# Pages ahead of the other loads in SyncE's queue, page products in halves around a step's clip, prepares at steps 14 and 18

## What is computed

```python
def stick_breaking_block(q, k, v, bias, q_pos, k_pos):
    z = (jnp.einsum('bqhd,bkhd->bhqk', q, k).astype(jnp.float32) * (SB_HEAD_DIM ** -0.5)
         + bias.astype(jnp.float32)[None, :, None, None])
    mask = k_pos[None, :] < q_pos[:, None]
    log_keep = jnp.where(mask, jax.nn.log_sigmoid(-z), 0.0)
    between = lax.cumsum(log_keep, axis=3, reverse=True) - log_keep
    a = jnp.where(mask, jnp.exp(jax.nn.log_sigmoid(z) + between), 0.0)
    return jnp.einsum('bhqk,bkhd->bqhd', a.astype(v.dtype), v)
...
    past_k = cache_sb_k[:, page_table].reshape(N_AB, n_seq, n_pages * PAGE_SIZE, SB_HEADS, SB_HEAD_DIM)
```

## Time and profile before

| | |
|---|---|
| median of 3 runs | 3360.61 us (3356.51 to 3362.72) |
| the profiled execution | 3363.24 us |
| its span in the trace | 3360.6 us |
| TensorE busy over the span | 2947.2 us (88%) |
| VectorE busy over the span | 1535.9 us (46%) |
| the stage of the change | about 564 to 938 us of the span |
| its mean TensorE clock | 0.76, 0.73 and 0.77 in pairs 0 to 2, 1.00 in pair 3 |

### The profile page before, as it was taken

One profiled execution on the slowest core, in us unless ns is written; L12 is line 12 of the kernel. 1 busy time (PEld: TensorE's weight loads), 2 busy tenths in 40 slices (PEclk: granted clock), 3 DMA queues, 4 the chain that ended last, 5 costly groups with the idle time before them and its releaser, 6 DMA issues. The chain is left out here.

```text
span 3360.6 us, 46161 instructions
## 1 busy us (share of the span) xinstructions
PE 2947.2 (88%) x17599; PEld 2570.9 (77%) x17599; DVE 1535.9 (46%) x1933; ACT 861.1 (26%) x1326; POOL 585.4 (17%) x504
## 2 busy tenths in 40 slices
PE   7999998987966888788888999999888998888887
PEld 7988887433436787788568999999777888888657
DVE  6276665777555673341424221111355642341423
ACT  5211113555751101220232100011232232120221
POOL 0002222554711221100011210000222301100011
PEclk9999998867987998899998999999887898989988
DMA  7379886776434002313541222222444453202641
GB/s 262 120 253 308 301 298 205 222 231 200 122 138 163 19 19 80 120 38 121 212 151 50 107 100 100 94 81 100 171 166 143 163 184 104 94 31 99 233 158 63
DMA packets 242194, 489.51 MB, mean 146 GB/s; under 512 B 37897, under 2 KB 98954, under 8 KB 241682
## 3 DMA queue, kind: packets, MB, share of 16 engines
q1 hardware_dynamic: 225298, 429.04, 38.0%
q0 software_dynamic: 12560, 43.07, 3.8%
q10 hardware_dynamic: 4176, 15.32, 1.1%
HBM read 378.83 MB, written 112.78 MB: 146 GB/s over the span
## 5 line engine op out<-in xcount | busy, mean ns | idle before, releaser
L414 PE MATMUL ps<-in_hi,w_hi 128*128 128x344 f32 x2496 | 806.4, 323 | 92.4 <-DVE in_lo L317 92.4
L415 PE MATMUL ps<-in_lo,w_hi 128*128 128x344 f32 x2496 | 803.8, 322 | 0.0
L416 PE MATMUL ps<-in_hi,w_lo 128*128 128x344 f32 x2496 | 802.8, 322 | 0.0
L414 PEld LDWEIGHTS ps<-in_hi,w_hi 128*128 128x128 f32 x2496 | 474.6, 190 | 96.2 <-DVE in_lo L317 96.2
L416 PEld LDWEIGHTS ps<-in_hi,w_lo 128*128 128x128 f32 x2496 | 474.7, 190 | 0.0
L415 PEld LDWEIGHTS ps<-in_lo,w_hi 128*128 128x128 f32 x2496 | 474.6, 190 | 0.0
L273 DVE CAST w_hi<-w_raw 128x1024 fp32r<-128x1024 f32 x64 | 49.5, 774 | 507.8 <-PE ps L416 495.0
L277 POOL TENSOR_TENSOR w_lo<-w_raw,w_hi 128x1024 fp32r<-128x1024 f32 x40 | 95.3, 2388 | 1024.9 <-ACT w_hi L273 1024.9
L1499 PE MATMUL ps<-in_hi,wv_hi 128*128 128x344 f32 x696 | 227.2, 326 | 2.1 <-DVE wv_lo L1349 2.1
L1500 PE MATMUL ps<-in_lo,wv_hi 128*128 128x344 f32 x696 | 223.1, 321 | 0.0
L1501 PE MATMUL ps<-in_hi,wv_lo 128*128 128x344 f32 x696 | 223.1, 321 | 0.0
(11 more groups left out here) (351 smaller groups left out, 5459.4 us busy)
## 6 DMA issues: line engine op xcount, KB each, us to landing
k_pages<-in_cache_k SPq DMA_DIRECT2D x256, 256.0 KB, 4.2
v_pages<-in_cache_v POOLq DMA_DIRECT2D x128, 256.0 KB, 5.1
v_pages<-in_cache_v SPq DMA_DIRECT2D x128, 256.0 KB, 3.0
cc<-stage SPq DMA_DIRECT2D x48, 516.0 KB, 2.7
w_raw<-in_w_c SPq DMA_DIRECT2D x48, 512.0 KB, 4.2
in_raw<-og SPq DMA_DIRECT2D x40, 516.0 KB, 5.6
kq_raw<-in_w_mem SPq DMA_DIRECT2D x32, 512.0 KB, 4.1
xs_kv<-in_mem_k SPq DMA_DIRECT2D x16, 1024.0 KB, 6.7
```

The source lines that it names most:

```text
L414: pe.matmul(o, w_hi[:, u, a:b], h, start=(kt == 0), stop=False)
L415: pe.matmul(o, w_hi[:, u, a:b], l, start=False, stop=False)
L416: return pe.matmul(o, w_lo[:, u, a:b], h, start=False, stop=(kt == KT - 1))
```

## The change

SyncE's queue: in each group j the k pages and then the v pages are issued first. The v tile follows the pages of j = 1, the store and the gate those of j = 2, and the next pair's heads are loaded one after the pages of j = 3 and one after those of j = 4. The eight products and eight reduces of a pair are cut into halves of 1024 columns: one half between softplus and clip of the step, the other after the clip. The semaphores count halves accordingly. The prepares move from steps 6 and 13 to steps 14 and 18.

```diff
--- before.py
+++ after.py
@@ -499,7 +499,7 @@
 PROD_AT = (0, 3, 5, 8, 10, 12, 15, 17)
 VALUES_AT = (3, 5, 7, 9, 11, 13, 15, 17)
 CLIP_AT, MASK_AT, COLUMNS_AT, SUFFIX_AT, SUMS_AT = 19, 19, 20, 21, 22
-PREP_AT = (6, 13)
+PREP_AT = (14, 18)
 VALUES_IN_AT = (13, 17)
 GATE_0_AT, GATE_1_AT = 10, 2
 
@@ -612,7 +612,7 @@
 
             def k_pages(p, j):
                 if NJ * p + j >= 2:
-                    sp.wait_ge(prod_done, NJ * p + j - 1)
+                    sp.wait_ge(prod_done, 2 * (NJ * p + j) - 2)
                 pages(cache_k, kp, kp_in, p + NW + 1, j)
 
             def v_pages(p, j):
@@ -622,18 +622,19 @@
 
             for p in range(PAIRS):
                 for j in range(NJ):
+                    if p + NW + 1 < S:
+                        k_pages(p, j)
+                    if p + NW < S:
+                        v_pages(p, j)
+                    if j == 1 and p + 1 < PAIRS:
+                        sp.wait_ge(vt_done, 2 * p + 2)
+                        sp.dma_start(vt[:, 0:T], ab[AB_V + 1 + p][:, 0:T]).then_inc(v_in, 16)
                     if j == 2:
                         if p:
                             store(p - 1)
                         sp.dma_start(gate[:, :], ab[AB_Z + p][:, 0:T]).then_inc(gate_in, 16)
-                        if p + 1 < PAIRS:
-                            for u in range(2):
-                                load_head(p + 1, u)
-                            sp.wait_ge(vt_done, 2 * p + 2)
-                            sp.dma_start(vt[:, 0:T], ab[AB_V + 1 + p][:, 0:T]).then_inc(v_in, 16)
-                    if p + 1 < PAIRS:
-                        k_pages(p, j)
-                    v_pages(p, j)
+                    if j in (3, 4) and p + 1 < PAIRS:
+                        load_head(p + 1, j - 3)
             sp.dma_start(s_gate[:, :, :], ab[AB_Z:AB_Z + 4, :, T:NT].rearrange("t p n -> p t n")).then_inc(s_gate_in, 16)
             sp.wait_ge(s_gated_done, 1)
             sp.dma_start(og[0:4, :, T:NT].rearrange("t p n -> p t n"), s_gated[:, :, :]).then_inc(s_stored, 16)
@@ -785,25 +786,27 @@
                 dve.tensor_tensor(gated[:, cols], ps[:, OB + c, :], gate[:, cols], ALU.mult).then_inc(og_done, 1)
 
             v3 = lambda x: x.rearrange("p (n h) -> p n h", h=SBH)
-            v4 = lambda x: x.rearrange("p (g n) -> p g n", g=G)
-
-            def product(p, j):
-                dve.wait_ge(kp_in[j % 2], 64 * (NJ // 2 * p + j // 2 + 1))
-                if NJ * p + j:
-                    dve.wait_ge(red_done, NJ * p + j)
-                s = p + NW + 1
-                dve.tensor_tensor(v4(prod[:, :]), v4(kp[:, j % 2, :]),
-                                  qbc[:, s:s + 1, :].broadcast_to((128, G, 512)), ALU.mult).then_inc(prod_done, 1)
-
-            def reduce(p, j):
-                dve.wait_ge(prod_done, NJ * p + j + 1)
+            v4 = lambda x: x.rearrange("p (g n) -> p g n", g=G // 2)
+
+            def product(p, j, half):
+                i = NJ * p + j
+                dve.wait_ge(kp_in[j % 2], 64 * (i // 2 + 1))
+                if i:
+                    dve.wait_ge(red_done, 2 * i + half - 1)
+                s, cols = p + NW + 1, slice(1024 * half, 1024 * half + 1024)
+                dve.tensor_tensor(v4(prod[:, cols]), v4(kp[:, j % 2, cols]),
+                                  qbc[:, s:s + 1, :].broadcast_to((128, G // 2, 512)), ALU.mult).then_inc(prod_done, 1)
+
+            def reduce(p, j, half):
+                dve.wait_ge(prod_done, 2 * (NJ * p + j) + half + 1)
                 if j == 0 and p:
                     dve.wait_ge(t_done, p)
-                dve.tensor_reduce(pz[:, j * G * SBH:(j + 1) * G * SBH], prod[:, :].rearrange("p (n d) -> p n d", d=SBD),
+                at, cols = (j * G + half * G // 2) * SBH, slice(1024 * half, 1024 * half + 1024)
+                dve.tensor_reduce(pz[:, at:at + G // 2 * SBH], prod[:, cols].rearrange("p (n d) -> p n d", d=SBD),
                                   k.AX.X, ALU.add).then_inc(red_done, 1)
 
             def page_clip(p):
-                dve.wait_ge(red_done, NJ * p + NJ)
+                dve.wait_ge(red_done, 2 * (NJ * p + NJ))
                 dve.scalar_tensor_tensor(v3(pz[:, :]), v3(pz[:, :]), SBD ** -0.5,
                                          bias_all[:, None, :].broadcast_to((128, NP, SBH)),
                                          ALU.mult, ALU.add).then_inc(zb_done, 1)
@@ -849,12 +852,16 @@
                     t = NS * p + s
                     if t + 1 < NT_:
                         softplus(t + 1)
+                    if s in PROD_AT and not last_pair:
+                        product(p, PROD_AT.index(s), 0)
+                    if s - 1 in PROD_AT and not last_pair:
+                        reduce(p, PROD_AT.index(s - 1), 0)
                     if t + 3 < NT_:
                         clip(t + 3)
                     if s in PROD_AT and not last_pair:
-                        product(p, PROD_AT.index(s))
+                        product(p, PROD_AT.index(s), 1)
                     if s - 1 in PROD_AT and not last_pair:
-                        reduce(p, PROD_AT.index(s - 1))
+                        reduce(p, PROD_AT.index(s - 1), 1)
                     if s == MASK_AT:
                         mask(p)
                     if s == CLIP_AT and not last_pair:
```

## The result

In 20 runs each the changed kernel took 3365.42 us in the median (3350.87 to 3374.32) and the kernel before 3352.93 (3345.0 to 3362.72): ratio 1.003, 95% interval 1.002 to 1.004. It is slower, by some 10 us by the ratio (12.5 between the medians), where 9.5 us of gain had been forecast. (The three runs of before known at the forecast, 3360.61 in the median, lay above the median of the 20.) The profiled execution of after took 3366.38 us, its span is 3364.2.

A forecast was written before the change was run, and what follows sets the result against it. The prediction took VectorE's k page waits and the near-bound issuing queue to bound the prompt attention; 16.7 + 2.4 + 2.4 - 12.0 = 9.5 us gained, off the median of 3360.61, gave 3351.0 us, range 3331 to 3366.

The forecast's parts named there:

- wait at step 5: VectorE's wait for k pages at the third page product of a pair, 26.1 us in three pairs, claimed to go.
- copy waits: VectorE waiting for ScalarE's k_stack copy, claimed as a sign: about 2.5 us at step 14 and about 1 at step 18.
- prepares at 14 and 18: Moving the prepares there was claimed to lengthen step 18 by 4.0 us in each of three pairs, 12.0 lost.
- queue order, up to product 5: Pages issued first were claimed to gain 8.1 us in pairs 1 and 2 each and 0.5 in pair 0, 16.7.
- steps 12 to 17 by VectorE's own work: Product 5 to the softplus of step 18, claimed 23.8 us against 24.6, for 2.4 us gained over three pairs.
- the first half fills the wait of the clip: A first half between softplus and clip was claimed to use up to 1.2 us of the clip's wait in a step.
- the tail: Steps 19 to 23 and on to the next clip of step 0; 2.4 us gained at step 0 in two pairs.
- The queue's chain: Issues one after another from v pages 2, claimed to put the last k pages of product 5 out by T0+44.1.
- T0+46.5: Claimed start of product 5 in pairs 1 and 2, in us after the start T0 of the pair's product 0.
- the wait that stays: Rival, chance 0.06: pages are themselves late, the wait remains, 12 us are lost and 4.8 gained, 3368.
- fixed costs eat the gain: Rival, chance 0.14: 0.16 us for each of 48 more instructions and 5.5 us per pair for prepares leave 0.3 gained, 3360.
- The low halves came late: Rival, chance 0.08: first product halves delay GpSimd's low halves and TensorE's suffix sum, 1.2 us in 24 steps, 3380.

## Why the prediction was wrong

*What was right.* The wait at step 5 is gone; waits at products 3 to 5 took its place, in an unbroken row of issues from v pages 2; the copy waits of 2.39 and 1.26 at steps 14 and 18 are the 2.4 and 1.2 of the forecast, and step 18 cost 3.8 where 4.0 was said. In pair 0 product 5 stands at 621.78, 1.2 us earlier than the 623 that was said. That the measured 3365.42 lies inside the range of 3331 to 3366 is luck: the range was laid around a median of before that was 7.7 us above that of the 20 runs.

By the parts that the runs took away one after the other, the sum failed in every term (its 16.7 also held what the prepares gone from step 6 and the first halves would give there):

| part | forecast | measured |
|---|---|---|
| prepares at 14 and 18 | -12.0 | -15.1 |
| queue order, up to product 5 | +16.7 | +8.3 |
| halves | +4.8 | -0.6 |
| sum | +9.5 | -7.5 |

By the pieces of a pair (the table further up) 14.3 of the 16.7 us had been gained by product 5 and were lost again behind it. There stand the steps that failed.

*The step that failed most: steps 12 to 17 by VectorE's own work, 23.8 us.* They took 26.5, 26.3 and 26.8 us; with what before took there, that is 8.9 of the 17.0 us by which the sum was wrong. In pair 0, 0.8 of the 2.7 is the clip of step 14 that waits for TensorE. The rest is GpSimd, for which I had counted nothing: the second product half of step 15 took 2.29 us (637.89 above) and those of step 17 took 1.81 and 1.63, where I put 1.22 each, 2.1 us in all; pair 1 has the same 2.1, pair 2 has 2.6. The product and reduce rows of after (minimum/median/maximum ns):

```profile
L797 DVE TENSOR_TENSOR prod<-k_pages,q_rows x48: 1206/1225/2290, 574.2 to 851.4; 128x1024 f32<-128x1024 f32 x48
...
L805 DVE TENSOR_REDUCE page_z<-prod x48: 1197/1202/1211, 577.2 to 856.0; 128x16 f32<-128x1024 f32 x48
```

A reduce half never leaves 1.2 us, a product half goes to 2.29. By the Trainium skill (SBUF — State Buffer, Who interferes with whom) a VectorE instruction with two SBUF inputs contends with a GpSimd one that reads SBUF, and a reduce never does; the trace agrees. The mean product rose from 2.490 to twice 1.448, by 0.41 us, where 0.16 was my upper bound; that halves simply meet GpSimd in more places is my reading of it. It is not the halves alone that make this piece long: with whole products and the same order and prepares it took 26.3, 25.8 and 26.3 us. What they failed to do is to bring it down to 23.8.

*The second: "the first half fills the wait of the clip", 4.8 us.* Filling VectorE's idle time moved the clip back for ScalarE and took the cover from the copy. In four pairs of kernels with and without halves the stage never got shorter: 2.4 us longer alone, 0.6 behind order and prepares, 1.8 with prepares at 11 and 16, 7.1 with the loads on ScalarE's queue. The first three are within what single landings do; the last is not. The further instructions by themselves lay inside the bounds of 0 to 7.7: measured 1.9. The Trainium skill (VectorE: DVE Perf Modes, The TRN2 errata) gives a fixed cost of about 150 cycles, which would be an estimated 0.16 us for each instruction; two reduce halves of 1.203 against a whole of 2.274 show 0.13, and the stage pays 0.04 for each of the 48.

*The third: nothing was taken off for the tail.* I let steps 19 to 23 stand as they were and even had 2.4 us gained there; 4.0 were lost, 2.7 of them in pair 0, where TensorE was granted 0.54 behind step 18. The same happened once in two other kernels with a prepare at 18: 0.56 behind it and 3.2 us lost in the tail of pair 1 with whole products and after's order, 0.57 and 2.6 us in pair 2 with prepares at 6 and 18. In the latter TensorE had been busy 6.04 of the 6.25 us of step 18, so its idle time in that step doesn't explain it.

*The queue's chain.* Product 5 came at T0+50.0 in pair 1 and T0+51.3 in pair 2, not at T0+46.5, which I had named as a sign of being wrong. In pair 1 v pages 2 left at T0+13.2 instead of T0+11.5, and from there to the last k page of product 5 it took 33.7 us instead of 32.6. Its waits were longer than the 2 to 4 us I had said: 5.94 at product 4, 2.93 and 3.63 at its neighbours. My sentence that the queue paces products 3 to 5 was right in effect and half wrong in cause, since a quarter of the issues left three fifths to two thirds of the waits.

*The bounds and the cases.* For the prepares I gave 2.5 to 5.5 us a pair and used 12 for three; the one line alone cost 15.1, inside these bounds (16.5). By its number the nearest case was the wait that stays (3368, given 0.06), but its mechanism did not come: no wait is left at step 5. By its mechanism the nearest was the one in which fixed costs eat the gain (0.14); its price was too short. The low halves came late in part: six took over 2 us, all beside products of steps 15 and 17 (four before), but TensorE's waits for them fell from 39.2 to 21.3 us.

*What stays open.* Why the clip of a kernel with prepares at 14 and 18 waits longer for TensorE as page waits are taken away (89.4 us against 82.1) is not settled; clocks in the stretch 574 to 845 are 0.76 and 0.77. Nor is what makes the clock fall behind some of the steps 18. And how much of each run's end is the landing of single pages: at the untouched first wait of pair 0 it was 5.2, 6.4, 8.2 and 7.9 us in four kernels of before's order with whole products (before and the three that move prepares only).

## What to carry to other kernels

A step that waits for another engine inside an in-order program should stand behind long work of its own engine: moving a prepare by one step, from behind a reduce to a step without one, added 6.6 us of waiting for the copy, most of what the reordered queue gained in this change (8.3). Loads for the next round belong where their queue stands idle; with that and the pages first, 7 to 8 tenths of a percent were gained, while in front of the pages or between them they cost waits either way. Splitting an instruction to fill an idle gap has to be priced with what its end covers on the other engines, not by VectorE's idle time alone.

## What the runs showed of the hardware that I had not expected

- A product half of 1024 columns took between 1.206 and 2.290 us beside GpSimd, a reduce half 1.197 to 1.211.
- A step 18 in which TensorE was busy 5.35 of 7.30 us at full clock (648.3 to 655.6) was followed by 15 us at a granted 0.56, one of 5.42 by 0.77, and in another kernel one of 6.04 of 6.25 by 0.57.
- One transfer of 1 MB landed 9.2 us after its issue in the median, a page of a fourth of that in 2.9 to 3.1, four of them issued in 3.63 us, one group every 4.41 us.
- Issues of 256 KB loads cost on ScalarE's queue what they cost on SyncE's, four in 2.40 us against 2.38; ScalarE had 10.1 us of issuing ahead of its own work in the stage.
